# Latent attention layer: keys before queries, in quarters of four heads, with the query norm taken as the scale of the exponential

## What is computed

```python
q_lat, kv_lat, k_rope = split_cols(h @ w_in, [256, 128, 32])
q = (rms_norm(q_lat, q_a_gain) @ w_q_b).reshape(B, L, 16, 96)
kv = (rms_norm(kv_lat, kv_a_gain) @ w_kv_b).reshape(B, L, 16, 64 + 64)
k_nope, v = split_cols(kv, [64, 64])
k = concatenate([k_nope, broadcast(k_rope to 16 heads)])
q = rms_norm(q, q_gain)          # over the 96 features of a head
k = rms_norm(k, k_gain)
q[..., 64:], k[..., 64:] = apply_rope(...)       # pairs (i, i+16), cos and sin of the position
logits = einsum('bqhd,bshd->bhqs', q, k) * 96 ** -0.5     # causal mask
out = einsum('bhqs,bshd->bqhd', softmax(logits), v) @ w_out
```

## Time and profile before

| quantity | value |
|---|---|
| median of three runs | 1852.52 us (1844.11 to 1853.59) |
| profiled execution, its own time | 1854.97 us |
| its span (first to last instruction) | 1853.2 us |
| PE busy | 1729.7 us, 93% |
| DVE busy | 1149.7 us, 62% |
| ACT busy | 933.7 us, 50% |
| POOL busy | 212.5 us, 11% |

### The profile page before, as it was taken

The page is one execution under the profiler, slowest core; times in us unless marked ns, Lnnn a source line. Parts: engine busy times, 40 slices in busy tenths (PEclk is TensorE's granted clock), DMA queues, the critical chain, the costliest instruction groups (busy, mean ns, idle before and its releaser), DMA issues.

```text
span 1853.2 us, 26443 instructions
## 1 busy us (share of the span) xinstructions
PE 1729.7 (93%) x9356; PEld 1460.5 (79%) x9356; DVE 1149.7 (62%) x1913; ACT 933.7 (50%) x1511; POOL 212.5 (11%) x287
## 2 busy tenths in 40 slices
PE   7999999999999997999997999993899999889998
PEld 6889988887788775788885788872598888669887
DVE  6677454555777748665667665555555664775565
ACT  5462355644455455644456544454744445465443
POOL 3005420100000015100007100002000000230000
PEclk9999999999999978999999999997999998799999
DMA  8440046556465532466663366643066664225662
GB/s 270 126 137 1 1 137 182 159 155 191 143 196 169 177 114 66 126 190 188 188 184 101 103 192 188 188 127 113 1 203 190 186 191 143 80 85 179 191 190 82
DMA packets 158176, 270.28 MB, mean 146 GB/s; under 512 B 15164, under 2 KB 41227, under 8 KB 158091
## 3 DMA queue, kind: packets, MB, share of 16 engines
q1 hardware_dynamic: 156571, 263.35, 46.2%
q0 software_dynamic: 1504, 5.79, 0.9%
q10 hardware_dynamic: 16, 0.00, 0.0%
HBM read 268.04 MB, written 1.07 MB: 145 GB/s over the span
## 4 chain that ended last, share of the span: by engine, by line
PE 82%; DVE 8%; ACT 4%; issue 3%; POOL 2%; DMA 0%; DVEq 0%; SPq 0%; ACTq 0%; POOLq 0%
PE p_AC L2376 11%; PE p_AC L2377 11%; PE p_AC L2378 11%; PE p_UP L2376 6%; PE p_UP L2378 6%; PE p_UP L2377 6%; PE p_TP L2409 5%; PE p_UP L2409 5%; PE p_TP L2443 3%; PE p_UP L2410 2%; PE p_TP L2410 2%; DVE t_wl L1907 1%; PE p_AC L1092 1%; PE p_UP L1080 1%; PE p_AC L1094 1%
## 5 line engine op out<-in xcount | busy, mean ns | idle before, releaser
L1907 DVE TENSOR_TENSOR t_wl<-t_raw,t_wh 128x1024 fp32r<-128x1024 f32 (+2 forms) x524 | 609.9, 1170 | 504.6 <-ACT t_wh L1333 502.2
L1333 ACT ACTIVATE t_wh<-t_raw 128x1024 fp32r<-128x1024 f32 (+2 forms) x524 | 529.1, 1016 | 603.0 <-PE p_AC L2378 290.8
L2376 PE MATMUL p_AC<-t_wh,t_uTh 128*128 128x512 f32 x612 | 243.3, 398 | 15.7 <-DVE t_wl L1907 8.8
L2377 PE MATMUL p_AC<-t_wl,t_uTh 128*128 128x512 f32 x612 | 241.5, 395 | 0.0
L2378 PE MATMUL p_AC<-t_wh,t_uTl 128*128 128x512 f32 x612 | 241.2, 394 | 0.0
L2376 PE MATMUL p_UP<-t_wh,t_hT 128*128 128x512 f32 (+3 forms) x576 | 227.3, 395 | 4.1 <-DVE t_hT L1952 4.0
L2378 PE MATMUL p_UP<-t_wh,t_hT 128*128 128x512 f32 (+3 forms) x576 | 224.0, 389 | 0.0
L2377 PE MATMUL p_UP<-t_wl,t_hT 128*128 128x512 f32 (+3 forms) x576 | 224.0, 389 | 0.0
L2376 PEld LDWEIGHTS p_AC<-t_wh,t_uTh 128*128 128x128 f32 x612 | 116.5, 190 | 42.4 <-DVE t_uTl L2069 8.0
L2409 PE MATMUL p_TP<-t_hT,t_wh 128*128 128x512 f32 x384 | 144.4, 399 | 0.0
L2409 PE MATMUL p_UP<-t_hT,t_wh 128*128 128x512 f32 x384 | 144.0, 398 | 0.0
(11 more groups left out here) (338 smaller groups left out, 2806.7 us busy)
## 6 DMA issues: line engine op xcount, KB each, us to landing
t_raw<-in_w_up SPq DMA_DIRECT2D x128, 512.0 KB, 4.0
t_raw<-in_w_down SPq DMA_DIRECT2D x128, 512.0 KB, 3.8
t_raw<-in_w_in SPq DMA_DIRECT2D x72, 512.0 KB, 3.7
t_raw<-in_w_up SPq DMA_DIRECT2D x88, 256.0 KB, 4.0
t_raw<-in_a_w_in SPq DMA_DIRECT2D x26, 512.0 KB, 3.9
t_raw<-in_w_down SPq DMA_DIRECT2D x44, 256.0 KB, 3.1
t_raw<-in_a_w_out SPq DMA_DIRECT2D x16, 512.0 KB, 3.4
t_raw<-in_b_w_in SPq DMA_DIRECT2D x12, 512.0 KB, 4.1
```

The source lines that it names most:

```text
L1333: A_(wh[:, c % SPL, 0:size(c)], raw[:, c % RAW, 0:size(c)], ACT.Copy).then_inc(high_done, 1)
L1907: V.tensor_tensor(wl[:, c % SPL, 0:n], raw[:, c % RAW, 0:n], wh[:, c % SPL, 0:n].bitcast(F32), ALU.subtract).then_inc(split_done, 1)
L2376: M(outs[t], a_hi, w_hi[:, k, :], start=first and k == 0, stop=False)
L2377: M(outs[t], a_hi, w_lo[:, k, :], start=False, stop=False)
```

## The change

The weights' order becomes lat, four key/value blocks, four query blocks of 384 columns (four heads each), output. Keys are finished first, quarter by quarter: sum of squares, power, scaled copy to a tile of their own (`K3`), 8 transposes to `TP`, one copy of 96 x 1024 by ACT. Query blocks are multiplied between the transposes of the key quarters. A query quarter is rotated without being scaled (its gains for the rotated part are folded into `rope_tab` beforehand), transposed, and copied by DVE (`query_copy_dve`). Its norm goes elsewhere: DVE multiplies the row maxima of a pair by the root `q_root`, and ACT takes the exponential with the negative root `neg_rq` as the scale in place of -1. The copies of query quarters 2 and 3, the sum of squares of quarter 3 and the transposes of quarter 3 are made within the core. The rests of the first output block's four chunks are made in steps 8 to 11 of the core; two of its high parts are made before the core, two in steps 8 and 9. The latent's transposes, high parts and rests go in two parts, the keys' tile first.

The diff, cut to its core (eight columns of indentation left out):

```diff
         b["lat"] = add_block(column_block(rows(c_w_in_2[n]), KD, 0, 416))
-        b["q"] = [add_block(column_block(rows(c_w_q_b_2[n]), 2, j * COLS, COLS)) for j in range(3)]
         b["kv"] = [add_block(column_block(rows(c_w_kv_b_2[n]), 1, j * COLS, COLS)) for j in range(4)]
+        b["q"] = [add_block(column_block(rows(c_w_q_b_2[n]), 2, j * 4 * QK3, 4 * QK3)) for j in range(4)]
...
+W3 = (slot(1, 768, 1024), hid[:, 0:768])
+KSQ = (hid[:, 0:512], hid[:, 512:1024])
+K3 = [v.rearrange("p (t h e) -> p t h e", t=NT, e=QK3)
+      for v in (slot(5, 768), slot(5, 768, 768), slot(3, 768), slot(3, 768, 768))]
+rot = slot(5, 512, 1536).rearrange("p (a t h i) -> p a t h i", a=4, t=NT, i=16)
+rope_tab = small(128).rearrange("p (a t i) -> p a t i", a=4, t=NT)
+neg_rq = small(32)
...
+def latent_act(act, A_, b, read_block, ahead, highs):
+    kv, q = b["kv"], b["q"]
+    out0 = b["out"][0]
+    ahead(kv[0])
+    highs(kv[1], 0, 1)
+    highs(kv[2], 0, 1)
+    read_block(b["lat"], lambda t: LAT[:, t, :], 416, r_tok, split_next=False)
     act.wait_ge(blk_free(gid(b["lat"])), gid(b["lat"]) // 2 + 1)
     n = 0
     for lo, hi in ((0, 256), (256, 384)):
@@ -641,30 +666,36 @@
                       accum_out=lat_ss[:, n:n + 1])
             n += 1
     last.then_inc(sem("ls_done"), 1)
+    for n, tiles in enumerate(((2,), (0, 1))):
+        upto(act, "lt_done", n + 1)
+        for k in tiles:
+            gain = g_cq + k if k < 2 else g_ckv
+            last = A_(uTh[:, k, :], TP[:, k * S:(k + 1) * S], ACT.Copy, scale=gains[:, gain:gain + 1])
+        last.then_inc(sem("lh_done"), 1)
+    highs(kv[3], 0, 1)
     upto(act, "lr_done", 1)
+
     for j in range(4):
+        if j >= 2:
+            upto(act, "ck_in", j - 1)
+        read_block(kv[j], lambda t: KV3[:, t, 4 * j:4 * j + 4, :].rearrange("p h e -> p (h e)"),
+                   COLS, lat_ss[:, 2:4], split_next=False,
+                   square=lambda t: (KSQ[j % 2][:, 256 * t:256 * t + 256].rearrange("p (h e) -> p h e", e=64),
+                                     bank(gid(kv[j]), t).rearrange("p (h e) -> p h e", e=P)[:, :, 0:64]))
+        highs(q[j], 0, 1)
+    for j in range(4):
+        upto(act, "k3_done", j + 1)
+        A_(feature_quarter(MK, j), TP[0:QK3, :], ACT.Copy, scale=gains[0:QK3, g_c3 + 1:g_c3 + 2])\
+            .then_inc(sem("k3c_done"), 1)
+        if j == 1:
+            upto(act, "ck_in", 4)
+        if j >= 2:
+            upto(act, "cq_in", j - 1)
+        w = 4 * QK3
+        read_block(q[j], lambda t: Q3[:, t * 1536 + j * w:t * 1536 + (j + 1) * w], w, lat_ss[:, 0:2],
+                   split_next=False,
+                   square=lambda t: (W3[j % 2][:, w * t:w * t + w], bank(gid(q[j]), t, w)))
+    highs(out0, 0, 2)
...
+def query_copy_dve(dve, V, j):
+
+    upto(dve, "q3_done", j + 1)
+    src = (AC[:, 2 * COLS:4 * COLS], AC[:, 2 * COLS:4 * COLS], TP[:, :], AC[:, 0:2 * COLS])[j]
+    V.tensor_scalar(feature_quarter(MQ, j), src[0:QK3, :], gains[0:QK3, g_c3:g_c3 + 1], None, ALU.mult)\
+        .then_inc(sem("q3c_done"), 1)
+
+def latent_dve(dve, V, link, b, ahead, rests):
+
+    kv, q = b["kv"], b["q"]
     csv = cs.rearrange("p (c t i) -> p c t i", c=2, t=NT)
     sin, cos = csv[:, 0], csv[:, 1]
     upto(dve, "cs_done", 1)
+    for a, (f, lo) in enumerate(((cos, 64), (sin, 80), (cos, 80), (sin, 64))):
+        V.tensor_tensor(rope_tab[:, a], f, rc_cq[:, lo:lo + 16].unsqueeze(1).broadcast_to([P, NT, 16]), ALU.mult)
+    ahead(kv[0])
+    rests(kv[1], 0, 1)
+    rests(kv[2], 0, 1)
+    evacuated(dve, b["lat"])
...
+    for n, tiles in enumerate(((2,), (0, 1))):
+        upto(dve, "lh_done", n + 1)
+        for k in tiles:
+            gain = g_cq + k if k < 2 else g_ckv
+            last = V.scalar_tensor_tensor(uTl[:, k, :], TP[:, k * S:(k + 1) * S], gains[:, gain:gain + 1],
+                                          uTh[:, k, :].bitcast(F32), ALU.mult, ALU.subtract)
+        last.then_inc(sem("ll_done"), 1)
+    rests(kv[3], 0, 1)
...
+    def key_sums(j):
+        evacuated(dve, kv[j])
+        link(V.tensor_reduce(k_root(j), KSQ[j % 2].rearrange("p (n e) -> p n e", e=64), AX, ALU.add))
+        V.scalar_tensor_tensor(per_head(k_root(j)), per_head(k_root(j)), 1.0 / QK3,
+                               krs.unsqueeze(2).broadcast_to([P, NT, 4]), ALU.mult, ALU.add)\
+            .then_inc(sem("ck_in"), 1)
+
+    def key_norm(j):
+        upto(dve, "ck_done", j + 1)
+        r = per_head(k_root(j)).unsqueeze(3)
+        V.tensor_tensor(K3[j][:, :, :, 0:64], KV3[:, :, 4 * j:4 * j + 4, 0:64],
+                        r.broadcast_to([P, NT, 4, 64]), ALU.mult)
+        V.tensor_tensor(K3[j][:, :, :, 64:96], ropek.unsqueeze(2).broadcast_to([P, NT, 4, ROPE]),
+                        r.broadcast_to([P, NT, 4, ROPE]), ALU.mult).then_inc(sem("k3_ready"), 1)
+
+    def query_sums(j):
+        evacuated(dve, q[j])
+        link(V.tensor_reduce(q_root(j), W3[j % 2].rearrange("p (n e) -> p n e", e=QK3), AX, ALU.add))
+        V.tensor_scalar(q_root(j), q_root(j), 1.0 / QK3, EPS, ALU.mult, ALU.add).then_inc(sem("cq_in"), 1)
+
+    def query_rope(j):
+        evacuated(dve, q[j])
+        h4 = slice(4 * j, 4 * j + 4)
+        for a, lo in enumerate((64, 80, 80, 64)):
+            last = V.tensor_tensor(rot[:, a], Q3v[:, :, h4, lo:lo + 16],
+                                   rope_tab[:, a].unsqueeze(2).broadcast_to([P, NT, 4, 16]), ALU.mult)
+        link(last)
+        V.tensor_tensor(Q3v[:, :, h4, 64:80], rot[:, 0], rot[:, 1], ALU.subtract)
+        V.tensor_tensor(Q3v[:, :, h4, 80:96], rot[:, 2], rot[:, 3], ALU.add).then_inc(sem("q3_ready"), 1)
+
+    key_sums(0)
+    rests(q[0], 0, 1)
+    key_sums(1)
+    key_norm(0)
+    rests(q[1], 0, 1)
+    key_sums(2)
+    key_norm(1)
+    rests(q[2], 0, 1)
+    key_sums(3)
+    key_norm(2)
+    rests(q[3], 0, 1)
+    key_norm(3)
+    query_rope(0)
+    query_sums(0)
+    query_rope(1)
+    query_copy_dve(dve, V, 0)
+    query_sums(1)
+    query_rope(2)
+    query_copy_dve(dve, V, 1)
+    query_sums(2)
+    query_rope(3)
...
+def query_quarter_pe(pe, transposes, j):
+
+    upto(pe, "q3_ready", j + 1)
+    dst = (AC[:, 2 * COLS:4 * COLS], AC[:, 2 * COLS:4 * COLS], TP[:, :], AC[:, 0:2 * COLS])[j]
+    transposes([(dst[0:QK3, (i * NT + t) * P:(i * NT + t + 1) * P], Q3v[:, t, 4 * j + i, :])
+                for i in range(4) for t in range(NT)], sem("q3_done"))
+
 def latent_pe(pe, M, transposes, b, block_mm):
+    kv, q = b["kv"], b["q"]
+
+    def key_quarter(j):
+        upto(pe, "k3_ready", j + 1)
+        if j > 0:
+            upto(pe, "k3c_done", j)
+        transposes([(TP[0:QK3, (i * NT + t) * P:(i * NT + t + 1) * P], K3[j][:, t, i, :])
+                    for i in range(4) for t in range(NT)], sem("k3_done"))
+
     block_mm(b["lat"])
     evacuated(pe, b["lat"])
+    for tiles in ((2,), (0, 1)):
+        transposes([(TP[:, k * S + t * P:k * S + (t + 1) * P], LAT[:, t, k * P:(k + 1) * P])
+                    for k in tiles for t in range(NT)], sem("lt_done"))
     upto(pe, "ll_done", 1)
+    for it in kv:
         block_mm(it, uTh, uTl, 2)
+    upto(pe, "ll_done", 2)
+    key_quarter(0)
+    block_mm(q[0], uTh, uTl, 0)
+    key_quarter(1)
+    block_mm(q[1], uTh, uTl, 0)
+    key_quarter(2)
+    query_quarter_pe(pe, transposes, 0)
+    block_mm(q[2], uTh, uTl, 0)
+    key_quarter(3)
+    upto(pe, "q3c_done", 1)
+    query_quarter_pe(pe, transposes, 1)
+    block_mm(q[3], uTh, uTl, 0)
+    upto(pe, "k3c_done", 4)
+    query_quarter_pe(pe, transposes, 2)
+    upto(pe, "q3c_done", 2)
...
+                if n == 2:
+                    upto(act, "mr_done", i + 1)
...
+                        r = head_t(h, t)
+                        last = A_(cols, cols, ACT.Exp, scale=neg_rq[:, r:r + 1] if n == 2 else -1.0,
+                                  bias=mx[:, k:k + 1], accum_out=esum[:, k:k + 1])
...
+            if n % 3 != 1 and PAIRS <= i < PAIRS + 2:
                 highs(blocks["out"][0], i - PAIRS + 2, i - PAIRS + 3)
...
+            for j in range(4):
+                upto(pool, "ck_in", j + 1)
+                pool.tensor_tensor(k_root(j), k_root(j), mhalf[:, 0:8], ALU.pow).then_inc(sem("ck_done"), 1)
+            for j in range(4):
+                upto(pool, "cq_in", j + 1)
+                link(pool.tensor_tensor(q_root(j), q_root(j), mhalf[:, 0:8], ALU.pow))
+                pool.tensor_scalar(neg_rq[:, 8 * j:8 * j + 8], q_root(j), -1.0, None, ALU.mult)\
+                    .then_inc(sem("cq_done"), 1)
...
+            if n == 2 and i == 2:
+                query_copy_dve(dve, V, 3)
...
+                if n == 2:
+                    if i == 0:
+                        query_copy_dve(dve, V, 2)
+                    upto(dve, "cq_done", i // 2 + 1)
+                    dve.wait_ge(max_done, hb + 2 * i + 2)
+                    both = mx_v[:, :, 2 * i:2 * i + 2]
+                    V.tensor_tensor(both, both, per_head(q_root(i // 2))[:, :, 2 * (i % 2):2 * (i % 2) + 2],
```

(28 more changed lines are left out.)

107 lines of the change are left out of this document (14 added, 93 removed).

## The result

The changed kernel takes 1823.63 us (median of 4 runs, 1818.10 to 1824.34), the kernel before 1853.05 (4 runs, 1844.11 to 1854.91): a ratio of 0.9855, 95% interval 0.9824 to 0.9887. A second lot of four runs gave 1820.98 (1814.01 to 1824.57) and 0.981, 0.9773 to 0.9847. The forecast was 1822, faster.

The account below looks back on a forecast made before the run. PE was busy 93% overall, so only stretches where it idles could shrink. First scores at 1277.4, core 26.3 + 4.0 + 0.5 + 0.8 = 31.6, output block at 1311.4 instead of 1342.8: 31.4 us saved, forecast 1822, range 1811 to 1833.

Parts of the forecast that it names:

- 11.4 us for PE's work: Before the core, from 1262.0: three query blocks (6.0 with matmuls and transposes together 11.4 us) and six transpose sets set the pace.
- eight hand-overs: Query part before the core: 0.25 us allowed for each of eight hand-overs, 2.0 us added.
- a stretch at the low clock: Query part before the core: one half-clock stretch in which 4 us do the work of 2, 2.0 us added.
- Rival (b): Query part before the core: PE stays at the low clock, +9.4 us, 1831.4 us in all; chance 10%.
- that is latency in a pipeline two steps deep, and I charge nothing: Core steps: ACT waits for both heads' maxima and their multiplication, about 0.9 us later in a step; charged nothing.
- DVE's additions: Core: two copies, a sum with mean and eight multiplications, 5.1 us of work; bounds 3 and 5.1, taken as 4.0.
- the operand: Core: ACT's exponentials take their scale from memory; 32 of them cost 0 to 3.0 us, taken as 0.5.
- the split: End of the core: one high part of 1.0 us on ACT stands ahead of the last probabilities' copies, +0.8 us.
- Rival (a): Core: turns DVE- and ACT-bound, each step stretched by 0.9, 7.2 us more, 1829 us; chance 14%.
- (c): Before and in the core: no low stretch, shorter hand-overs, cheaper DVE and ACT additions, 4.8 us less, 1817.2 us; chance 12%.
- (d): Before the core: quarters don't overlap, stretch 84 to 97 us, kernel slower by 23 to 36, about 1883 us; chance 3%.
- (e): Norm as scale brings no saving because DVE was never full; scaling only moves into the core; no separate chance given.

Follow-up runs that it names:

- the kernel with the copies first: Changed kernel, with ACT copying the probabilities of pair i-2 ahead of the exponentials of pair i in the core: 1819.88 us.
- later splits: Changed kernel, with two high parts of the output block made in steps 9 and 10 instead of 8 and 9: 1821.31 us.
- without the norm: Changed kernel, probabilities copied before exponentials, with neither multiplication of the maxima nor scale operand, queries left unnormalised: 1813.04 us.
- the run that undid it: Changed kernel, with queries multiplied by their norm before rotation and no norm in the core: 1831.68 us, ratio 0.9893 to the kernel before.
- the filled wait: Changed kernel, probabilities copied before exponentials, plus seven unused matmuls in PE's first wait in the core: 1818.37 us.
- order and splits: Changed kernel, probabilities copied before exponentials, and two high parts of the output block made one step later: 1818.84 us.

## Why the forecast was right, and where it was not

*The start and the keys.* Right. PE's first key block at 1248.50 (forecast 1248.5); ACT took the key blocks out from 1250.23 to 1260.60 (1250.5 to 1260.9); PE's second key transposes at 1261.91 (1262.0), behind the new wait for ACT's copy, 1.92 us.

*The query quarters.* The step "11.4 us for PE's work" held: 11.9. The two additions to it did not: of the 2.0 for eight hand-overs 0.5 came in all, and the 2.0 for a stretch at the low clock did not occur there, the granted clock being 1.00 throughout. The low stretch came in the core, where nothing was charged for it. With them the first scores were forecast 3.6 too late, the first maximum 3.3.

*Transposes and the clock.* Rival (b) fell: 48 transposes and 36 matmuls in turn ran at 1.00. The rule of the Trainium skill in "TensorE: Matmul & The Clock Gate", Part 4, that a transpose doesn't count as activity for the clock gate, would have led to the low clock here. This stretch alone doesn't refute it, for matmuls stood between; the earlier trace rows does more, with transposes only from 1297 to 1301, behind which the clock was granted at 0.98.

*The core.* The failed step is "that is latency in a pipeline two steps deep, and I charge nothing". The forecast looked at how busy DVE and ACT are and asked whether their work fits into a step. It didn't ask what stands *behind* the waiting instruction on ACT: the copies that free `TP` for PE. That was 3.4 us with the low clock in the same place and 4.65 in the run that also had it sooner; the core missed its forecast by 4.0. In the kernel with the copies first the core is 30.9, near the forecast's 26.3 + 4.0 + 0.5 + 0.8 = 31.6. But the single terms hold only in part: DVE's additions 2 x 1.28, 0.94, 0.17 and eight of 0.16 are 5.0 as records; the first four steps grew by 3.0 with the clock full (13.05 against 10.02) where 4.0 were taken for DVE; the norm with its scale operand is 0.9 where 0.5 was taken for the operand. The tail grew by 0.9 (7.99 against 7.05) where 0.8 was taken for the split, but in this order that is not the split's doing: later splits leave it at 7.97, and without the norm it is 7.40. Only in the old order was the split worth its 0.7. And the low stretch, at nothing in the sum, cost about 1.4 in the changed kernel, and with the order mended 0.7 or, where it lay later, 2.0 (15.01 against 13.05).

*The rivals.* Rival (a), the pairs handed back and forth, had the right place and named the mechanism's first half, with 7.2 us; the norm was worth 3.5. It was thought of as too much work, where 2.6 of the 3.5 were the order. (c) was right for the stretch in front of the core. (d) did not come: PE, busy 22.3 of 29.2 us there, overlaps with DVE at 22.5 and ACT at 25.2. Nor did (e): the norm as scale is worth 6.6 us by the run that undid it, some of them the clock's.

*The signs.* Of those named, PE's waits (1.92 at most) and the clock in front of the core (1.00) came as said. Three missed: the first scores 29.4 us after the last `lat` matmul (32 to 36 said), the core 35.6 (31), the middle steps 3.54 (3.2 to 3.4). The core stayed 0.4 below the 36 at which the forecast called itself wrong.

*The sum.* 3.3 better in front, 4.0 worse inside: the output block at 1312.1 instead of 1311.4. The time was right to 1.6 us because two errors of the same size had opposite signs, not because each step was.

*A better version.* The order of ACT alone takes 4.65 us off this stretch (3.4 by the order, the rest by where the low clock fell), with the filled wait 5.3. In times, each against the kernel before in the same lot, the changed kernel stands at 0.9855 and 0.981, the one with the order at 0.982 (0.9788 to 0.9852), order and splits at 0.9825 (0.9799 to 0.9852), order and filled at 0.9853 (0.9814 to 0.9892). The intervals overlap: that the new order is faster is shown by the stretch, not by the times, which the 9.4 us behind the output block can outweigh.

## What to carry to other kernels

When a wait is added to an engine that works strictly in order, ask first what stands behind it in that queue and who waits for that; moving an instruction that is already ready ahead of the wait gave 3.4 to 4.65 us here, while taking work off DVE, without it, made the core 1.6 longer. Put first what frees a buffer for the bound engine, then what feeds it. And a forecast of a sum is tested only by its parts: compare each stretch, or two errors that cancel teach nothing. Look at the granted clock of both stretches before a difference is put down to an edit.
